# FFN gate/up products with the weights stationary and 256 tokens moving, in a two-layer fp32 decoder trunk

## The reference

```
x = x + 0.5 * swiglu(rmsnorm(x, g1), w1_gate, w1_up, w1_down)
p = rmsnorm(x, g2) @ w_in        # 4 heads of differential attention, 4 of retention
x = x + concat(attention, retention) @ w_out
x = x + 0.5 * swiglu(rmsnorm(x, g3), w2_gate, w2_up, w2_down)
swiglu(h) = (silu(h @ w_gate) * (h @ w_up)) @ w_down      # 1024 -> 2816 -> 1024
rmsnorm(x, g) = x * rsqrt(mean(x*x, -1) + 1e-6) * g
```

## Time and profile before

| | |
|---|---|
| median of 3 runs | 993.77 us (993.65 to 994.35) |
| span of the profiled execution | 992.8 us |
| TensorE matmul (PE) busy | 965.0 us, 97% |
| weight loads (PEld) busy | 796.2 us, 80% |
| VectorE (DVE) busy | 547.3 us, 55% |
| ScalarE (ACT) busy | 455.8 us, 46% |
| GpSimd (POOL) busy | 39.7 us, 4% |
| DMA | 178.70 MB, mean 180 GB/s |

### The profile page before, as it was taken

The page is one execution under the profiler, slowest core; times in us unless marked ns, Lnnn a source line. Parts: engine busy times, 40 slices in busy tenths (PEclk is TensorE's granted clock), DMA queues, the critical chain, the costliest instruction groups (busy, mean ns, idle before and its releaser), DMA issues.

```text
span 992.8 us, 12951 instructions
## 1 busy us (share of the span) xinstructions
PE 965.0 (97%) x4512; PEld 796.2 (80%) x4512; DVE 547.3 (55%) x628; ACT 455.8 (46%) x579; POOL 39.7 (4%) x73
## 2 busy tenths in 40 slices
PE   2999999999999999999999999999999999999997
PEld 2888888888888888888878888888888888888885
DVE  3654545565666645454655545456565755454454
ACT  3634344454573534343453434343655554343432
POOL 3400000000010000000000000000001000000000
PEclk9999999999999999999999999999999999999999
DMA  9664646447245655556536655656634645656541
GB/s 251 219 208 160 208 161 206 171 160 241 91 164 170 205 199 172 208 169 211 188 131 214 188 193 175 205 171 210 209 110 165 213 134 189 212 165 207 164 141 43
DMA packets 123179, 178.70 MB, mean 180 GB/s; under 512 B 5664, under 2 KB 95776, under 8 KB 123136
## 3 DMA queue, kind: packets, MB, share of 16 engines
q1 hardware_dynamic: 121808, 173.56, 52.4%
q0 software_dynamic: 1040, 3.54, 1.5%
q10 hardware_dynamic: 288, 1.05, 0.3%
HBM read 177.08 MB, written 1.05 MB: 179 GB/s over the span
## 4 chain that ended last, share of the span: by engine, by line
PE 95%; DMA 1%; ACT 1%; issue 1%; DVE 1%; SPq 0%; ACTq 0%; POOLq 0%; DVEq 0%; POOL 0%
PE gu L722 20%; PE gu L724 20%; PE gu L723 20%; PE acc L724 10%; PE acc L723 10%; PE acc L722 10%; PE tp L792 2%; DMA raw<-in_w_up_dram 1%; PE tp L737 1%; PE tp L840 1%; PE acc L851 1%; PE tp L863 1%; ACT w_hi L294 0%; ACT wide L394 0%; PE acc L863 0%
## 5 line engine op out<-in xcount | busy, mean ns | idle before, releaser
L478 DVE TENSOR_TENSOR w_lo<-raw,w_hi 128x2048 fp32r<-128x2048 f32 (+1 forms) x168 | 376.2, 2243 | 158.5 <-ACT w_hi L294 158.3
L722 PE MATMUL gu<-w_hi,xT_hi 128*128 128x512 f32 x896 | 353.1, 394 | 11.4 <-DVE w_lo L478 11.0
L724 PE MATMUL gu<-w_hi,xT_lo 128*128 128x512 f32 x896 | 350.2, 391 | 0.0
L723 PE MATMUL gu<-w_lo,xT_hi 128*128 128x512 f32 x896 | 349.7, 390 | 0.0
L294 ACT ACTIVATE w_hi<-raw 128x2048 fp32r<-128x2048 f32 (+1 forms) x168 | 313.8, 1872 | 21.8 <-DMA raw<-in_w_up_dram 11.4
L722 PEld LDWEIGHTS gu<-w_hi,xT_hi 128*128 128x128 f32 x896 | 168.8, 188 | 46.7 <-issue 12.3
L336 ACT ACTIVATE hid<-gu,st 128x256 f32<-128x256 f32 x88 | 41.8, 475 | 352.2 <-PE gu L724 352.1
L724 PEld LDWEIGHTS gu<-w_hi,xT_lo 128*128 128x128 f32 x896 | 168.7, 188 | 35.7
L723 PEld LDWEIGHTS gu<-w_lo,xT_hi 128*128 128x128 f32 x896 | 168.9, 189 | 34.1
L722 PE MATMUL acc<-w_hi,aT_hi 128*128 128x512 f32 x384 | 157.0, 409 | 0.0
L534 DVE SCALAR_TENSOR_TENSOR hid<-gu,st,hid 128x256 f32<-128x256 f32 x88 | 42.5, 483 | 205.3 <-ACT hid L336 205.3
(11 more groups left out here) (111 smaller groups left out, 396.4 us busy)
## 6 DMA issues: line engine op xcount, KB each, us to landing
raw<-in_w_gate_dram SPq DMA_DIRECT2D x88, 512.0 KB, 4.0
raw<-in_w_up_dram SPq DMA_DIRECT2D x88, 512.0 KB, 5.0
raw<-in_w_down_dram SPq DMA_DIRECT2D x88, 512.0 KB, 4.3
raw<-in_w_in_dram SPq DMA_DIRECT2D x40, 512.0 KB, 4.6
raw<-in_w_out_dram SPq DMA_DIRECT2D x16, 512.0 KB, 3.7
raw<-in_w_in_dram SPq DMA_DIRECT2D x16, 256.0 KB, 3.0
gain<-in_norm_ffn_dram POOLq DMA_DIRECT2D x3, 512.0 KB, 4.0
gain<-in_norm_mix_dram POOLq DMA_DIRECT2D x2, 512.0 KB, 4.8
```

The lines of the kernel that those rows point to most:

```text
L478: nc.vector.tensor_tensor(w_lo[:, pos % SLOTS, 0:n], raw[:, pos % RAW, 0:n], w_hi[:, pos % SLOTS, 0:n].bitcast(F32), ALU.subtract).then_in ...
L722: nc.tensor.matmul(out_, s_hi, m_hi, start=first, stop=False)
L723: nc.tensor.matmul(out_, s_hi, m_lo, start=False, stop=False)
L724: return nc.tensor.matmul(out_, s_lo, m_hi, start=False, stop=last)
```

## The change

In steps 1 to 10 of each FFN the roles are exchanged. A piece now holds only gate or only up weights (128 x 8 x 256). The weights are stationary, 128 hidden columns at a time, and the 256 tokens move: `half_up` does 48 matmuls with 256 moving columns for the gate, into `gu[0]`, and as many for up, into `gu[1]`. The result has the hidden columns on the partitions, so the transposes of these steps go. `rstd` now varies along the free axis: GpSimd stores it to a small DRAM tensor and loads it back into all partitions (`spread_rstd`, once per FFN); VectorE multiplies the gate by it, ScalarE takes the Silu, VectorE multiplies by the unscaled up product, ScalarE makes `aT_hi`, VectorE `aT_lo`, each in one instruction of 128 x 512. The `rstd` that belongs to up is applied after the down product: `residual` uses `half_r` = 0.5 `rstd` in place of 0.5, and GpSimd makes that in `entry`. Step 0 keeps its form, without `rstd` on up.

```diff
-                if len(srcs[0].shape) == 3 and srcs[0].shape[1] == 4:
+                if side_by_side:
...
             def load_gu(it, pos, j):
+                for i, w in enumerate((wg, wu)):
+                    rows = [w[layer, h * 512:(h + 1) * 512, bass.ds(j * CH, CH)].rearrange("(k p) n -> p k n", p=P)
+                            for h in range(2)]
+                    load(layer, it, base + pos + i, rows)
...
@@ GpSimd, entry @@
+            pool.wait_ge(rstd_done, TT * q + tt + 1)
+            nc.gpsimd.tensor_scalar(half_r[:, tt:tt + 1], rstd[:, tt:tt + 1], 0.5, None, ALU.mult).then_inc(half_done, 1)
+            def spread_rstd(layer, f):
+                i = 2 * layer + f
+                pool.wait_ge(r_bc_loaded, 16 * i)
+                pool.dma_start(r_row, rstd).then_inc(r_row_stored, 16)
+                pool.wait_ge(r_row_stored, 16 * i + 16)
+                pool.dma_start(r_bc[:, :], r_row.rearrange("p t -> (p t)").partition_broadcast(P)).then_inc(r_bc_loaded, 16)
...
@@ ScalarE, a step @@
-                    silu(s_, 0, it, pos)
-                    nxt(0)
-                    silu(s_, 1, it, pos)
-                    hidden_hi(2 * s_, par, 0)
-                    nxt(1)
-                    hidden_hi(2 * s_ + 1, par, 1)
-                    nxt(2)
+                    act.wait_ge(gate_scaled, w0 + s_ + 1)
+                    nc.scalar.activation(gate_r, gate_r, ACT.Silu).then_inc(wsilu_done, 1)
+                    nxt(0)
+                    act.wait_ge(whid_done, w0 + s_ + 1)
+                    nc.scalar.activation(aT_hi[:, 2 * par:2 * par + 2, :], hiddenT, ACT.Copy).then_inc(wT_hi_done, 1)
+                    nxt(1)
+                    nxt(2)
...
@@ VectorE, residual @@
+                    if factor != 1.0:
+                        dve.wait_ge(half_done, TT * (q - 1) + tt + 1)
...
@@ VectorE, a step @@
+                    if pos == 2:
+                        dve.wait_ge(r_bc_loaded, 16 * i + 16)
+                        dve.wait_ge(hT_psum, 2 * i + 2)
+                    dve.wait_ge(slot_free, SLOTS + LP * layer + SLOTS * it + base + pos + 1)
+                    nc.vector.tensor_tensor(gate_r.rearrange("p k (t n) -> p k t n", t=TT), gu[0][:, :].rearrange("p (k t n) -> p k t n", k=2, t=TT),
+                                            r_bc[:, :].rearrange("p (n t) -> p t n", t=TT).unsqueeze(1).broadcast_to([P, 2, TT, P]),
+                                            ALU.mult).then_inc(gate_scaled, 1)
+                    nxt(0)
+                    dve.wait_ge(wsilu_done, w0 + s_ + 1)
+                    dve.wait_ge(slot_free, SLOTS + LP * layer + SLOTS * it + base + pos + 2)
+                    nc.vector.tensor_tensor(hiddenT, gu[1][:, :].rearrange("p (k n) -> p k n", k=2), gate_r,
+                                            ALU.mult).then_inc(whid_done, 1)
+                    nxt(1)
+                    dve.wait_ge(wT_hi_done, w0 + s_ + 1)
+                    lo_of(aT_lo[:, ks, :], hiddenT, aT_hi[:, ks, :], wT_lo_done)
+                    nxt(2)
...
@@ TensorE @@
+            def half_up(it, pos, bank, hook=None):
+                piece_ready(layer, base + pos, it)
+                slot = (base + pos) % SLOTS
+                for m in range(2):
+                    for k in range(KT):
+                        if hook and (m, k) == (1, 0):
+                            hook()
+                        ws = slice(k * CH + m * P, k * CH + (m + 1) * P)
+                        ins = three(bank[:, m * SEQ:(m + 1) * SEQ], w_hi[:, slot, ws], w_lo[:, slot, ws],
+                                    xT_hi[:, k, :], xT_lo[:, k, :], k == 0, k == KT - 1)
+                ins.then_inc(slot_free, 1)
+            def up(s_, it, pos, hook=None):
+                if hook is None:
+                    pe.wait_ge(gate_scaled, w0 + s_)
+                half_up(it, pos, gu[0], hook)
+                if hook is None:
+                    pe.wait_ge(whid_done, w0 + s_)
+                half_up(it, pos + 1, gu[1])
...
                 p_ = FFN_PIECES - 4
+                up(STEPS - 1, 0, p_)
+                for tt in range(TT):
+                    down((wT_lo_done, w0 + STEPS - 1), 0, p_ + 2, 1, tt)
                     if tt:
                         enter_T(q + 1, 0)
+                    down((wT_lo_done, w0 + STEPS), 0, p_ + 3, 0, tt, last=True)
```

More of the change, by code:

```diff
@@ L86, in build @@
         ident = sb("ident", [P, P])
+        r_bc = sb("r_bc", [P, SEQ])
+        r_row = nc.dram_tensor("r_row", (P, TT), F32, kind="Internal").ap()
         lams = qT[:, 0:2, :].rearrange("p a (b n) -> p (a b) n", b=2)
@@ L273, in mixer_and_ffn2_entry @@
                     entry(3 * layer + 2, tt)
+                spread_rstd(layer, 1)
             next_gain(0, norm_mix[0, :])
@@ L365, in ffn @@
                 act.wait_ge(rstd_done, TT * (3 * layer + 2 * f) + TT)
-                step(s0, 0, 0, 1, pieces(0, 3, 4, None))
-                step(s0 + 1, 1, 0, 3, pieces(0, 5, 6, 7))
+                first_step(pieces(0, 3, 4))
+                step(1, 1, pieces(0, 5, 6, 7))
                 with act.Fori(0, LOOPED) as it:
@@ L370, in ffn @@
                         p_ = 8 + 3 * u
-                        step(s0 + 2 * it + 2 + u, u, it, 6 + 3 * u, pieces(it, p_, p_ + 1, p_ + 2))
-                step(s0 + STEPS - 1, 0, 0, FFN_PIECES - 3, last_lots)
+                        step(2 * it + 2 + u, u, pieces(it, p_, p_ + 1, p_ + 2))
+                step(STEPS - 1, 0, last_lots)
             def head_squares(n, src, done):
@@ L510, in residual @@
                             dve.wait_ge(slot_free, SLOTS + used)
-                        nc.vector.scalar_tensor_tensor(x[:, tt, cols], acc[2 * tt + half][:, :], factor, x[:, tt, cols],
+                        by = 1.0 if factor == 1.0 else half_r[:, tt:tt + 1]
+                        nc.vector.scalar_tensor_tensor(x[:, tt, cols], acc[2 * tt + half][:, :], by, x[:, tt, cols],
                                                        ALU.mult, ALU.add).then_inc(x_new, 1)
@@ L543, in step, with first_hide @@
-                def step(e, par, it, nxt):
-                    hide(e, 0)
-                    nxt(0)
-                    hide(e + 1, 1)
-                    hidden_lo(e, par, 0)
-                    nxt(1)
-                    hidden_lo(e + 1, par, 1)
+                i = 2 * layer + f
+                w0 = (STEPS - 1) * i - 1
+                def first_hide(tt):
+                    dve.wait_ge(silu_done, 2 * i + tt + 1)
+                    nc.vector.tensor_tensor(hidden[:, tt, :], gu[tt][:, CH:2 * CH], silu_g[:, tt, :], ALU.mult).then_inc(hidden_done, 1)
@@ L563, in ffn @@
                 split_lo(layer, base + 2)
-                step(e0, 0, 0, pieces(0, 3, 4, None))
-                step(e0 + 2, 1, 0, pieces(0, 5, 6, 7))
+                first_step(pieces(0, 3, 4))
+                step(1, 1, 0, 2, pieces(0, 5, 6, 7))
                 with dve.Fori(0, LOOPED) as it:
@@ L568, in ffn @@
                         p_ = 8 + 3 * u
-                        step(e0 + 4 * it + 4 + 2 * u, u, it, pieces(it, p_, p_ + 1, p_ + 2))
-                step(e0 + 2 * (STEPS - 1), 0, 0, last_lots)
+                        step(2 * it + 2 + u, u, it, 5 + 3 * u, pieces(it, p_, p_ + 1, p_ + 2))
+                step(STEPS - 1, 0, 0, FFN_PIECES - 4, last_lots)
             def mixer(layer):
@@ L778, in ffn, with first_T @@
             def ffn(layer, f, base):
-                e0 = 2 * STEPS * (2 * layer + f)
+                i = 2 * layer + f
+                w0 = (STEPS - 1) * i - 1
                 q = 3 * layer + 2 * f
[L782 to L790, removed]
+                def first_T(tt):
+                    pe.wait_ge(hidden_done, 2 * i + tt + 1)
                     for k in range(2):
@@ new lines, in up, with down @@
+                def up(s_, it, pos, hook=None):
[5 more added lines that the diff above has]
+                    half_up(it, pos + 1, gu[1])
+                def down(ready, it, pos, par, tt, **kw):
+                    pe.wait_ge(*ready)
+                    add_rows(layer, it, tt, base + pos, aT_hi, aT_lo, 2 * par, **kw)
@@ L804, in ffn @@
+                project(layer, 0, 0, base, 2, gu_ready, lambda: enter_T(q, 1), q)
+                project(layer, 0, 1, base, 2, gu_ready, None, q)
+                first_T(0)
+                up(1, 0, 2, lambda: first_T(1))
                 for tt in range(TT):
-                    hidden_T(e0 + 2 + tt, tt)
-                    down(e0 + tt, 0, 4, 0, tt, first=True)
+                    down((hT_lo_done, 2 * i + tt + 1), 0, 4, 0, tt, first=True)
                 with pe.Fori(0, LOOPED) as it:
@@ L808, in ffn @@
                     for u in range(2):
-                        e = e0 + 4 * it + 4 + 2 * u
+                        s_ = 2 * it + 2 + u
+                        up(s_, it, 5 + 3 * u)
                         for tt in range(TT):
[L811 to L815, removed]
@@ L816, in ffn @@
-                for tt in range(TT):
```

(5 more changed lines are left out.)

70 lines of the change are left out of this document (39 added, 31 removed).

## The result

1022.67 us (median of 4 runs, 1022.52 to 1023.32) against 994.06 us before, measured beside it: ratio 1.0295, 95% interval 1.028 to 1.0309. The forecast was 999.5 us. The direction was right, the size was not; the time is that of the rival with the fixed price (1024 us).

A forecast was written before the change was run, and what follows sets the result against it. TensorE's streaming and waits were taken to bound the kernel: 992.8 us, less 20.4 for the stream, plus 26.1 for three waits with the clock's fall, gave 998.5 of span; 1.0 more for the median, 999.5. Range 984 to 1030.

The forecast's parts named there:

- the rival with the fixed price: Gate/up stream: the 0.0133 us surcharge is paid per instruction, 0.120 us a 256-column matmul; 1024 us in all; chance 0.28.
- What bounds the kernel, and where it could be hurt: Whole kernel: TensorE is busy 97% of the span, so its streaming and any place where it would wait count.
- The price of a matmul with 256 columns: Gate/up products in the 40 exchanged steps: 0.1133 us each, half of 0.2266, making the stream term -20.4 us.
- The inference from L863: fp32 products at 0.111 us an instruction, 0.005 over their columns, were taken to show no fixed cost of 0.013.
- The two readings: Price of a 256-column gate/up matmul: 0.1133 us by columns (-20.4 us in all) or 0.120 per instruction (+5.2).
- my case's own range: Whole kernel: price near 0.1133 us with three waits and the clock's fall, 991 to 1006 us; chance 0.42.
- The transposes' 0.51 us a step: Middle steps: the four removed transposes and what they disturb cost 0.51 us a step, saved in 40 steps.
- The wait in the last step: Last step of three of four FFNs: TensorE waits 6.0 us for the hidden tile's low part, behind a split.
- the rival with the longer gate/up: Matmul price 0.120 us: the last-step wait is 0.3 us shorter, 8.4 a place with the clock; chance 0.28.
- The clock: After each of the three last-step waits: 5.8 us at the lower clock level, 2.7 us lost each.
- Middle steps, r_bc, the half factor: Other engines' work in middle steps, the spread rstd's transfer and GpSimd's extra instruction: hidden, costing nothing.
- The shared feed: Gate/up stream: moving and stationary columns share one feed, 0.136 us a matmul; 1083 us; chance 0.08 (or worse).

The follow-up runs named there:

- run 5: Not the decoder: a kernel of matmul runs alone, varying moving columns, stationary columns and type; 256 fp32r took 120 ns, 512 took 228, 256 bf16 109.
- run 9: Not the decoder: fp32r matmuls alone with 96, 64, 32 stationary columns, or alternating lengths; 256 moving columns took 116, 114, 114 ns, an alternating pair 347.
- run 1: Changed kernel, but in an FFN's last step VectorE makes the hidden tile's low part before splitting the next phase's second piece; 1007.5 us, ratio to before 1.0143.
- run 2: Changed kernel with both splits of the next phase's pieces behind the hidden tile's low part in the last step; 1008.5 us, ratio to before 1.0149.
- run 6: Changed kernel with both next-phase splits behind the low part, VectorE's second one behind the first tile's residual; 1000.73 us, ratio to before 1.0076.
- run 3: Changed kernel plus 20 unread 512-column matmuls on TensorE ahead of its last-step wait in three FFNs; 1015.88 us, ratio to before 1.0227.
- run 8: As run 7, but each half's eight 512-column matmuls come first, then its eight of 256; 988.35 us, ratio to before 0.9946.
- run 7: As run 6, but in steps 2 to 9 high-by-high and high-by-low products share one 512-column matmul; 994.86 us, ratio to before 1.0014.
- run 4: Kernel before, old roles and transposes kept, each 512-column gate/up matmul made as two of 256; 1021.93 us, ratio to before 1.0283.

## Why the prediction was right in its direction and wrong in its size

- *What bounds the kernel, and where it could be hurt:* right. TensorE has no gap in the middle steps of the changed kernel either (155.00 us busy from 35 to 190), and all the loss is in its stream and its waits.
- *The price of a matmul with 256 columns:* the step that failed. I took 0.1133, in proportion, for the reason that "a pair has no fixed cost of 0.013 on top of its columns"; it is 0.120, the upper bound that I named for a price per instruction. The term came out as +6.0 us and not -20.4: 26.4 us more, where the span was missed by 22.4 (1020.9 for 998.5), as the waits and the clock cost 4 us less than I had summed. The runs' median was missed by 23.2: it stands 1.8 above the profiled span and not 1.0. The result is inside the range of 984 to 1030, but only because that took in the rival with the fixed price. The inference from L863 was the fault. That product is plain fp32, which takes two instructions a matmul, each as long as twice its columns; run 5 shows it at 256 columns (218 ns an instruction) and run 9 at L863's own 128 (L76: 3.57 / 32 = 112 ns), both 5 ns over that, where fp32r is 13 over. It was the nearest row by duration and not by type. The rows of the fp32r matmuls themselves held only one length, so they could not separate a price per instruction from one per column. The two readings stood 26 us apart, as much as all the waits together, and nothing in the trace decided between them; my case's own range, 991 to 1006, claimed more.
- *The transposes' 0.51 us a step:* right; 96 x 0.120 - 48 x 0.2266 - 0.51 = +0.13 was the rival's sum, and the step grew by 0.15.
- *The wait in the last step:* right in place, cause and count: three waits, for L529's low part behind a split, none in the last FFN. 5.3 us each where the sum had 6.0; the rival with the longer gate/up said 5.7. Runs 1, 2 and 6 show that the order of the splits is the cause. The split named is 4.0 of the 5.3; the other 1.3 are VectorE's two splits ahead of the up product (run 1).
- *The clock:* right. It fell at all three, and cost 2.0 us a place by the profile and 2.1 to 2.3 by run 3, where I took 2.7. The lower level lasted 3.4 to 6.8 us, but part of that lay in the waits, where it costs nothing.
- *Middle steps, r_bc, the half factor:* right to cost nothing. When VectorE comes to the second FFN's first scaling it waits for the gate product and not for r_bc:

```profile
344.20 0.69 DVE L593 TENSOR_TENSOR hid<-gu,r_bc 128x512 f32<-128x512 f32 x1 [0.98 <-PE gu L778]
```

- *The shared feed* (136 ns) is refuted by the 120 here, as the Trainium skill's rule of independent read ports has it (TensorE: Matmul & The Clock Gate, Part 2: What happens when you issue a matmul). The same page's N / 2.4 + 2.5 ns (Back-to-back issue gap), which it gives for a matmul by itself, is exact in run 5 for bf16 with a load for each, 109 and 56 ns, and 11 ns short for fp32r.
- *Sum of the measured terms:* 6.0 + 16.0 + 6.0 = 28.0 us, the span's 28.1.

## What to carry to other kernels

Count matmul instructions and not only columns: an fp32r matmul with its load of 128 columns pays 13 to 16 ns at every length measured (256 to 512), so halving the length to remove a few transposes can cost more than they did. Merging products that share a stationary operand into one long matmul gains: run 8, grouped by length, is 12.4 us under run 6. When the bounds of one price lie on both sides of no change, take the evidence of the same data type, or say that it is open. And when a result that used to come in halves now comes whole and late, read the program of every engine between it and its user: one split ahead of one instruction cost 4 us three times here, and the clock's fall added some 2 us to each.

## What the runs showed of the hardware that was not expected

- fp32r pays 13 to 16 ns a matmul with its load at the upper clock, for 256 to 512 columns; bf16 2.5, and at the lower clock nothing is seen (427 ns for 512).
- With 64 or 32 stationary columns the surcharge falls to 7 ns at 256 moving columns and rises to 17 or 18 at 512 (runs 5 and 9). Unexplained.
- The same matmuls in another order differ: 353 against 346 ns a pair in the decoder, 6.5 us of the kernel (runs 7 and 8).
- The granted clock did not fall at one fixed time after the stream stopped: 2.4 us after the last matmul before, but some 4.6, 5.1 and 2.2 us into the three waits here. Three waits of 1.3 us (run 1) did not bring it down. In run 2 a wait of 1.1 us and one of 0.7 close behind it come at the end of three FFNs: near 209 and 507 us the clock stayed up, near 700 it fell, for 3.4 us. In run 4 it fell 0.8 us after the end of a stop of 1.9 us, also for 3.4 us.
